# Two fused layers on one core: retention in plain fp32, a later start of layer 2's attention, and differential attention's TensorE work regrouped

## The reference, cut to what matters

```python
# retention, 8 heads, dk 64, dv 128, 4 chunks of 128 positions
def step(state, inp):
    qi, ki, vi = inp
    scores = einsum('bhnd,bhmd->bhnm', qi, ki) * inner_decay
    out = einsum('bhnm,bhme->bhne', scores, vi) + einsum('bhnd,bhde->bhne', qi, state) * q_decay
    state = state * chunk_decay + einsum('bhmd,bhme->bhde', ki * k_decay, vi)
# differential attention, 8 heads, two maps of dk 64, causal, 128 queries a block
s = einsum('bqhjd,bkhjd->bhjqk', qb, kb) - slopes * dist
p = softmax(s); a = p[:, :, 0] - lam * p[:, :, 1]
out = einsum('bhqk,bkhe->bqhe', a, vb)
# layer 2: 8 dilated heads (dk 64) and 8 latent heads (64 + 32), causal, then
mixed = concatenate([o_a * silu(z_a), o_b * silu(z_b)]); out = x + mixed @ w_out
```

## Time and profile before

| | |
|---|---|
| median of 3 runs | 1011.0 us (1006.83 to 1011.19) |
| profiled execution | 1010.72 us, its span 1008.9 us |
| TensorE busy | 966.0 us (96%) |
| VectorE, ScalarE, GpSimd busy | 439.3, 417.3, 479.1 us |
| mean granted TensorE clock | 0.988 |

### The profile page before, as it was taken

How to read it: one execution, slowest core, us unless ns; L and a number is a source line. 1 busy time by engine, 2 the same in 40 slices (tenths; PEclk the granted TensorE clock), 3 DMA queues, 4 the chain that set the end, 5 groups by cost and what they waited for, 6 DMA issues and landing times.

```text
span 1008.9 us, 13340 instructions
## 1 busy us (share of the span) xinstructions
PE 966.0 (96%) x4876; PEld 780.9 (77%) x4876; DVE 439.3 (44%) x1030; ACT 417.3 (41%) x912; POOL 479.1 (47%) x452
## 2 busy tenths in 40 slices
PE   6999998999999999999999999999899979999998
PEld 5777788876888877777767887789788857777777
DVE  3300367323211534567465523325656574456431
ACT  5333453323223344454455332226535354455431
POOL 3543542543446644654434433443457827634342
PEclk9999997999999999999999999999999989999999
DMA  6332210332333322222221241222224311100013
GB/s 212 105 87 82 84 43 1 85 97 70 102 91 101 104 84 67 63 81 64 64 59 47 84 167 63 97 91 80 85 66 132 106 54 50 44 21 22 21 30 117
DMA packets 41168, 78.71 MB, mean 78 GB/s; under 512 B 3296, under 2 KB 5088, under 8 KB 41104
## 3 DMA queue, kind: packets, MB, share of 16 engines
q1 hardware_dynamic: 40240, 76.30, 25.1%
q10 hardware_dynamic: 864, 1.57, 0.6%
HBM read 75.74 MB, written 2.12 MB: 77 GB/s over the span
## 4 chain that ended last, share of the span: by engine, by line
PE 80%; DVE 8%; ACT 4%; issue 3%; POOL 3%; DMA 1%; SPq 1%; ACTq 0%; DVEq 0%; POOLq 0%
PE Z L1671 22%; PE Z L1673 21%; PE Z L1672 20%; PE A L1901 4%; POOL w_lo L858 2%; PE A L1909 2%; PE A L1803 2%; PE A L1816 2%; PE A L1671 1%; DMA raw<-in_w_in 1%; PE A L1681 1%; PE A L1673 1%; PE A L1672 1%; PE A L1869 1%; ACT w_hi L529 1%
## 5 line engine op out<-in xcount | busy, mean ns | idle before, releaser
L858 POOL TENSOR_TENSOR w_lo<-raw,w_hi 128x512 fp32r<-128x512 f32 (+1 forms) x262 | 342.2, 1312 | 422.8 <-ACT w_hi L529 422.5
L1671 PE MATMUL Z<-w_hi,hT_hi 128*128 128x512 f32 (+1 forms) x832 | 339.2, 408 | 10.5 <-POOL w_lo L858 3.9
L1673 PE MATMUL Z<-w_hi,hT_lo 128*128 128x512 f32 (+1 forms) x832 | 324.7, 390 | 0.0
L1672 PE MATMUL Z<-w_lo,hT_hi 128*128 128x512 f32 (+1 forms) x832 | 324.5, 390 | 0.0
L529 ACT CAST w_hi<-raw 128x512 fp32r<-128x512 f32 (+1 forms) x262 | 158.3, 614 | 280.9 <-PE Z L1673 263.9
L1671 PEld LDWEIGHTS Z<-w_hi,hT_hi 128*128 128x128 f32 x832 | 157.0, 189 | 54.8 <-issue 8.8
L1673 PEld LDWEIGHTS Z<-w_hi,hT_lo 128*128 128x128 f32 x832 | 156.8, 188 | 33.0
L1672 PEld LDWEIGHTS Z<-w_lo,hT_hi 128*128 128x128 f32 x832 | 157.4, 189 | 26.7
L1671 PE MATMUL Z<-w_hi,oT_hi 128*128 128x512 f32 x128 | 51.6, 403 | 3.3 <-DVE tmp L1164 2.2
L684 ACT ACTIVATE x_sb<-x_sb,nmax 128x128 f32<-128x128 f32 (+3 forms) x64 | 35.5, 557 | 38.3 <-DVE nmax L1356 38.3
L1673 PE MATMUL Z<-w_hi,oT_lo 128*128 128x512 f32 x128 | 50.1, 391 | 0.0
(11 more groups left out here) (277 smaller groups left out, 1507.5 us busy)
## 6 DMA issues: line engine op xcount, KB each, us to landing
raw<-in_w_in SPq DMA_DIRECT2D x92, 512.0 KB, 3.8
raw<-in_w_out SPq DMA_DIRECT2D x16, 512.0 KB, 3.6
raw<-in_ret_w_o SPq DMA_DIRECT2D x8, 512.0 KB, 3.3
raw<-in_diff_w_o SPq DMA_DIRECT2D x8, 512.0 KB, 3.4
x_sb<-in_x SPq DMA_DIRECT2D x8, 256.0 KB, 5.3
x_sb<-in_x SPq DMA_DIRECT2D x4, 512.0 KB, 6.5
out<-x_sb SPq DMA_DIRECT2D x8, 256.0 KB, 3.3
raw<-in_w_in SPq DMA_DIRECT2D x4, 416.0 KB, 3.2
```

Of the source, the lines that this page charges most:

```text
L858: pool.tensor_tensor(w_lo[:, s % SPLIT_SLOTS, 0:width], raw[:, c % RAW_SLOTS, s - CHUNK_START[c], 0:width], w_hi[:, s % SPLIT_SLOTS, 0:wid ...
L1671: pe.matmul(out, l_hi, r_hi, start=first, stop=False)
L1672: pe.matmul(out, l_hi, r_lo, start=False, stop=False)
L1673: return pe.matmul(out, l_lo, r_hi, start=False, stop=last)
```

## The change

Retention: every split goes away. Turned queries and keys, decayed keys, masked scores, states and values are used as plain fp32, each product is one fp32 `pe.matmul`, `ret_f`, `st_f` and `kd_f` get two buffers, and ACT alone takes the turned queries and keys out of PSUM. Zeros for the query halves are written to two tiles, not four. Layer 2's attention begins after six slots (`ATT_WAIT`), its 71 steps are spread over 52 slots up to slot 57 instead of 57 slots up to slot 56; the six norm pieces move into DVE's steps 3 to 8, and DVE's part of a turned query or key moves to the head of its step. Differential attention: TensorE's step begins with `scores(n+1)`, followed by turn and outputs; the extra yield around `diff_turn` is dropped on all engines, and `diff_due` goes to 72 instead of 86.

```diff
-        return 36 * (v - DIFF_FIRST + 1) // (DIFF_SECOND - DIFF_FIRST)
+        return 29 * (v - DIFF_FIRST + 1) // (DIFF_SECOND - DIFF_FIRST)
     if v < DIFF_THIRD:
-        return 36 + 22 * (v - DIFF_SECOND + 1) // (DIFF_THIRD - DIFF_SECOND)
-    return min(86, 58 + 28 * (v - DIFF_THIRD + 1) // (DIFF_LAST - DIFF_THIRD))
-ATT_STEPS, ATT_SLOTS = 71, 57
+        return 29 + 17 * (v - DIFF_SECOND + 1) // (DIFF_THIRD - DIFF_SECOND)
+    return min(72, 46 + 26 * (v - DIFF_THIRD + 1) // (DIFF_LAST - DIFF_THIRD))
+ATT_STEPS, ATT_WAIT, ATT_SLOTS = 71, 6, 58
 def att_due(v):
-    if v < 0:
+    if v < ATT_WAIT:
         return 0
-    return min(ATT_STEPS, -(-ATT_STEPS * (v + 1) // ATT_SLOTS))
+    return min(ATT_STEPS, -(-ATT_STEPS * (v + 1 - ATT_WAIT) // (ATT_SLOTS - ATT_WAIT)))
...
 # ACT, retention: values, decayed_keys, masked_scores and states are removed
                 def turned_q(p):
                     act.wait_ge(r_t, turn_job("q", p) + 1)
                     for hh in range(2):
                         rows = slice(RDK * hh, RDK * (hh + 1))
-                        act.copy(ret_queries(p)[0][rows, hh, :], A[2][rows, :]).then_inc(r_hi, 1)
+                        last = act.copy(ret_queries(p)[rows, hh, :], A[2][rows, :])
+                    last.then_inc(r_turned, 1)
...
 # DVE, retention: turned_q, turned_k, values and the low parts are removed
-                            if p:
-                                dve.wait_ge(r_plo, 2 * p - 1 + i)
+                            if p > 1:
+                                dve.wait_ge(r_i, 2 * p - 3 + i)
                             dve.wait_ge(r_s, 2 * p + i + 1)
-                            dve.tensor_tensor(ret_f[:, i, :, :, :],
+                            dve.tensor_tensor(ret_f[:, p % 2, i, :, :, :],
...
 # PE, retention (scores; updates, inner and cross products alike)
-                            last = mm3(A[i][:, 256 * (c % 2):256 * (c % 2 + 1)], kT_hi[:, sl, cc], kT_lo[:, sl, cc],
-                                       q_hi[:, :, cc], q_lo[:, :, cc], True, True)
+                            last = pe.matmul(A[i][:, 256 * (c % 2):256 * (c % 2 + 1)], rk[:, p % 2, cc], q[:, :, cc],
+                                             start=True, stop=True)
...
-                    pe.wait_ge(r_slo, po + 1)
+                    pe.wait_ge(r_sf, po + 1)
...
 # DVE, layer 2's attention
                 for n in range(ATT_STEPS):
+                    if n >= 2 and turned_at(n - 2):
+                        att_qk(*turned_at(n - 2))
                     if n < N:
                         scores(n)
...
-                    if n >= 2 and turned_at(n - 2):
-                        att_qk(*turned_at(n - 2))
+                    if 3 <= n < 9:
+                        next(late)
...
 # PE, differential attention
                 for n in range(N + 4):
                     h, i = divmod(n, 4)
+                    if n + 1 < N:
+                        scores(n + 1)
                     if 0 <= n - LAG < N:
                         turn_probs(n - LAG)
                     if 0 <= n - 3 < N and i != 3:
                         outputs(n - 3)
                     yield
                     if i in (1, 2) and h + 1 < H:
                         diff_turn(h + 1, i - 1)
-                        yield
-                    if n + 1 < N:
-                        scores(n + 1)
                     if 0 <= n - 3 < N and i == 3:
                         outputs(n - 3)
                     yield
```

More of the change, by code:

```diff
@@ L596, in turned_q @@
                         rows = slice(RDK * hh, RDK * (hh + 1))
-                        act.copy(ret_queries(p)[0][rows, hh, :], A[2][rows, :]).then_inc(r_hi, 1)
+                        last = act.copy(ret_queries(p)[rows, hh, :], A[2][rows, :])
+                    last.then_inc(r_turned, 1)
                 def turned_k(p):
                     act.wait_ge(r_t, turn_job("k", p) + 1)
[L601 to L609, removed]
-                    if p:
[L611 to L626, removed]
+                    act.activation(rk[:, p % 2, :], A[2][:, :], ACT.Copy, scale=RDK ** -0.5).then_inc(r_turned, 1)
                 pairs = RH // 2
                 if stage == 1:
+                    act.wait_ge(q_zeros, 2)
                     turned_q(0)
@@ L1232, in scale_heads, with retention @@
                     dve.tensor_tensor(o, o, r, ALU.mult).then_inc(o_normed, 1)
[L1234 to L1241, removed]
-                def turned_k(p):
-                    dve.wait_ge(r_khalf, p + 1)
-                    dve.scalar_tensor_tensor(kT_lo[:, p % 2, :], A[2][:, :], RDK ** -0.5, kT_hi[:, p % 2, :],
-                                             ALU.mult, ALU.subtract).then_inc(r_lo, 1)
-                def values(p):
-                    vh, vl = ret_values(p)
-                    dve.wait_ge(r_vhi, p + 1)
-                    dve.tensor_tensor(vl, z_ret[:, :, 1024 + 256 * p:1280 + 256 * p], vh, ALU.subtract).then_inc(r_v, 1)
+            def retention():
                 def states(p):
                     dve.wait_ge(r_u, p + 1)
-                    if p:
-                        dve.wait_ge(r_slo, p)
+                    if p > 1:
+                        dve.wait_ge(r_x, 2 * (p - 1))
+                    st = st_f[:, p % 2, :, :]
                     for c in range(3):
@@ L1280, in retention @@
                 pairs = RH // 2
-                if start:
-                    turned_q(0)
-                    turned_k(0)
-                    values(0)
-                    return
                 for p in range(pairs + 1):
@@ L1297, in retention @@
                                               ALU.mult).then_inc(r_pf, 1)
[L1298 to L1307 removed]
                     if p == 0:
[L1309 to L1311 removed]
+                        states(p)
                     if p:
@@ L1433, in query_zeros, with attention @@
                     last.then_inc(q_zeros, 1)
-            def attention():
+            def attention(late):
                 ph, N = ATT2, 8 * H
@@ L1477, in attention, with att_slot @@
                     yield
-            def att_slot(g, k, steps, gates, late):
+            def att_slot(g, k, steps, gates):
                 v = TT * (KD * (g - G_ATT2) + k)
                 for t in range(TT):
-                    if v + t < 6:
-                        next(late)
                     if 30 <= v + t < 36:
@@ L1591, in _ @@
             dve.engine_nop().then_inc(cols_ready, 1)
-            steps, steps2, gates, late = diff(), attention(), take_gates(G_ATT2, 2), late_norms()
+            steps, steps2, gates = diff(), attention(late_norms()), take_gates(G_ATT2, 2)
             norms = {G_DIFF0 + 2: head_scale(HEAD_NORM[G_DIFF0 + 1]), G_DIFF0 + 3: head_scale(HEAD_NORM[G_DIFF0 + 2]),
@@ L1628, in _ @@
                     dve.engine_nop().then_inc(lam_dots, 1)
-                    for part in (*ret_queries(0), *ret_queries(1)):
+                    for part in (ret_queries(0), ret_queries(1)):
                         for hh in range(2):
@@ L1640, in _ @@
                                       ALU.add).then_inc(row_ready, 1)
-                if g == G_RET0:
-                    retention(start=True)
                 if g == G_RET:
@@ L1648, in _ @@
                     dve.wait_ge(row_out, 16)
-                    retention(start=False)
+                    retention()
                 if g == G_LAT:
@@ L1770, in retention @@
                             cc = slice(P * c, P * (c + 1))
-                            last = mm3(Z[2 + hh][:, cc], q_hi[:, hh, cc], q_lo[:, hh, cc],
-                                       st_hi[:, c - 1, :], st_lo[:, c - 1, :], True, True)
+                            last = pe.matmul(Z[2 + hh][:, cc], q[:, hh, cc], st_f[:, po % 2, c - 1, :], start=True, stop=True)
                         last.then_inc(r_x, 1)
```

124 lines of the change are left out of this document (34 added, 90 removed).

## The result

Before 1008.9 us (median of 4), after 1028.6 us (median of 4, 1027.9 to 1033.4): ratio 1.021, 95% interval 1.016 to 1.025. The forecast was 991 (984 to 1001). The profiled execution took 1028.5 us (span 1026.7). Parts A and B together take off 19.4 us against 17.7 forecast; part C, forecast at -2.7, costs 37.9.

What follows compares the result with a forecast made beforehand. The prediction took one nearly always full in-order TensorE queue as the bound, except at retention's end and layer 2's attention start. Its sum was 1010.7 - 14.7 - 3.0 - 2.7 = 990.3, said as 991, range 984 to 1001.

Steps and rivals of the forecast that it cites:

- Part A: Retention unsplit into single fp32 matmuls: -12.3 us at its end and -2.4 of clock behind it, -14.7; bounds -7 and -17.
- rival 3: Retention: fp32 matmuls of 256 columns cost like 512, +14 us, giving 1004; chance 0.03.
- rival 1: Retention's end: clock falls again or the tail stays on turns and copies, saving only 7 to 8 us, 998; chance 0.19.
- Part B: Layer 2's attention six slots later, with its VectorE and GpSimd reordering: -3 us; bounds +2 and -7.
- the slots that I priced at -3.6: Layer 2's attention start: idle 8.1 us against 7.4, but 12 slots done instead of 6, worth 4.5; net -3.6.
- the order of VectorE's query parts, priced at -0.5: Layer 2's attention: VectorE's query parts ahead of the scores help some key turns, -0.5 us.
- The 3.1 us in the turn of set 4: Layer 2's attention: TensorE waits up to 3.1 us there because GpSimd's first latent piece stands before set 4's scaling.
- Part C: Differential steps in one go, scores first on TensorE: -2.7 us; bounds +1 and -5.
- The +0.5 for the turn behind the low part: Differential stage: a query or key turn has one gap, not two, to the next turn of probabilities; +0.5 us.
- The term of -2.2: Differential stage: in 22 steps scores and turns share one excursion from the projection, saving 0.10 us each, -2.2.
- The -1.0: Differential stage: the second half's first key turn, waiting 1.5 us for z_sb, comes a slot or two later; -1.0 us.
- Rival 4: Differential stage: after 14 query and key turns the turn of probabilities waits for VectorE's low part, +32 us, 1022; chance 0.04.

Runs made afterwards that it cites:

- e10: e6 with layer 2's attention starting at slot 0 again over 57 slots, other edits of that attention kept: 990.8 us.
- e11: e6 with VectorE's low parts of layer 2's turned queries and keys back behind the row maximum and copy of the step: 995.2 us.
- e1: The changed kernel with the old differential step put back on every engine, the retention and layer 2 edits kept: 990.7 us.
- e6: The changed kernel with its pace of 72 half steps, but the scores back in the second half step, behind the query or key turn: 989.6 us.
- e7: The changed kernel with only VectorE's order changed: row maximum of set n+1 at the end of its first half step n, ahead of the low part: 996.4 us.
- e8: e7 with TensorE's first half step ordered turn, outputs, then scores of set n+1: 1001.7 us.
- e12: e6 with GpSimd's last six latent pieces one in a step from step 16 on, instead of two in each of steps 16 to 18: 988.3 us.

## Why the prediction was wrong, by its own steps

**Part A, -14.7 forecast, -14.5 measured.** The timeline of TensorE in retention's end after, for the earlier trace rows:

```profile
134.04 1.89 PE L1612 MATMUL A<-rq,rk 128*128 128x256 f32 x8
135.76 1.95 PE L1657 MATMUL Z<-z_ret,ret_f 128*128 128x128 f32 x16
137.55 0.60 PE L1599 MATMUL A<-ident,z_ret 128*128 128x128 f32 x4
...
141.19 0.70 PE L1626 MATMUL A<-z_ret,kd_f 128*128 128x256 f32 x2 [0.40 <-ACT rq L589]
...
148.87 0.70 PE L1626 MATMUL A<-z_ret,kd_f 128*128 128x256 f32 x2 [0.40 <-ACT rq L589]
...
158.43 0.50 PE L1573 MATMUL Z<-w_hi,hT_hi 128*128 128x512 f32 x1 [0.78 <-DVE o_sb L1228]
```

Four fp32 matmuls of 256 columns take 135.76 - 134.04 = 1.72, so 0.43 each (I took 0.45: rival 3 is out); eight of 128 columns take 1.79, 0.22 each. The hand-made schedule forecast waits of 0.4, 0.4 and 1.1; they are 0.40, 0.40 and 0.78. The end takes 24.4 (forecast 25.2), and the clock held: rival 1 is out. That the medians agree to 0.2 is partly luck: the windows give 37.5 - 24.4 = 13.1 at the end and 2.4 behind it, 15.5 in all. And the prediction's "agrees" for 0.223 rests on no row at 128 columns, where the fp32 matmul takes only twice the 0.11 of an fp32r one; at 512 columns it does take four times as long, 0.95 against 0.23.

**Part B, -3 forecast, -4.9 measured, for the wrong reason.** The waits at its start were right: 1.36 and 0.23 for Z2 and Z3, 3.00 for q_lo. But the slots that I priced at -3.6 are worth about 1, within the spread (e10), and the order of VectorE's query parts, priced at -0.5, is worth 5.5, as much as the whole of B (e11). (By its own terms, 8.1 - 7.4 - 4.5, the -3.6 should read -3.8. Part A's bound with the clock falling as before is -6.3 by its terms, not -7.) The 3.1 us in the turn of set 4 was a misreading of the diff: GpSimd's latent pieces begin in its step 10, not ahead of the scaling of set 4. They cost 2.3 + 0.8 = 3.1 later, where two pieces stand ahead of one scaling. GpSimd's timeline, then TensorE's:

```profile
875.62 2.66 POOL L890 TENSOR_TENSOR m_sb<-z_sb,lam_v 128x512 f32<-128x512 f32 x2
878.38 0.58 POOL L936 TENSOR_SCALAR sgd_sb<-sgd_sb,rinv 128x384 f32<-128x384 f32 x1
```

```profile
879.02 0.55 PE L1805 MATMUL A<-ident,sgd_sb 128*128 128x128 f32 x3 [1.36 <-POOL sgd_sb L936]
```

That the sign agreed, and the size roughly, is chance.

**Part C, -2.7 forecast, +37.9 measured: the step that failed.** It was "Scores leave half a step earlier, so exp, the weight copies queued behind it on ACT, and w_lo behind those wait less". I followed who is served earlier and not what the scores themselves wait for, so their wait for the row maximum stood in the sum at nothing. The runs showed 29.0 us of it, 27.7 more idle time over the same work, and 11.2 of busy time at a lower clock on top. The one wait for a row maximum in the stage before, 0.4 us, showed only that the old place was late enough; how late it had to be was in the same trace, in the time at which each row maximum ends. The +0.5 for the turn behind the low part looked at the right chain (1.8 us of turn, copy, low part), but the scores meet it first, with a row maximum of 0.7 to 1.3 added and norms between. In the 12 waits behind a low part at most four instructions stand between it and the row maximum that ends them.

The term of -2.2 had its count right and its price wrong. From the first scores to the last outputs TensorE returns to the projection 80 times in e1, 66 in e6 and 57 in the changed kernel and in e7, each return with 0.32 instead of 0.23 to the next matmul: 23 returns for the 22 forecast, which would be 2.1 us. But TensorE's busy time for that work is 193.0 in e1, with one slot of 0.7 more in it, 192.4 in e6 and 191.6 in e7, so 0.7 us is all that shows. The -1.0 held: the wait of 1.5 for z_sb is 0.3 in e6 and gone in the changed kernel.

**The rivals.** Rival 4 had the right sign and stage and a size of the right order (+32), and it named VectorE behind with other work; it named the wrong waiting instruction (e8 shows that one, 5.6 us). It got 0.04 because the stage before was idle for only 3.5 us and VectorE busy for half of it. Both rows were true and no evidence: e7 has the same VectorE work as the changed kernel and 26.4 us less of waits at the scores. No other rival had part C costing time.

**The version that beats both.** e6 (989.6), or e12 (988.3): parts A and B with TensorE's old order, 1.8% under the kernel before and 3.8% under the changed one.

## What to carry to other kernels

When an instruction is moved earlier in a full in-order queue, write down each thing that it waits for and walk the producer's queue up to it: everything that stands there between the old and the new place, with its own waits, becomes idle time of the full engine and of all that is queued behind. A stage with almost no idle time says that the present order has enough slack, not how much; the old trace says how much, in the time between the end of what an instruction waits for and the place to which it moves (511.55 against 508.90 above). Move the work that frees the bank first (here VectorE's row maximum), and only then the producer's.

## What was not expected of the hardware

The waits cost clock as well. After the wait of 3.34 us at 412.49 the projection's matmuls start 0.43 apart, and 0.23 apart again from 417.2 on; the chain of work that ended last and the window:

```profile
412.49 0.62 PE A L1700 x6
...
414.31 0.43 PE Z L1573
414.74 0.43 PE Z L1574
...
417.23 0.24 PE Z L1574
```

```profile
414.00:417.00 3.00, 3.00 (x9) 2.42 (x9) 2.69 (x13) 0.00 (x0) 0.00 (x0) 0.50 0.45 163
```

The granted clock there is 0.50, the lower level, 1.2 GHz. There are eight such falls in the stage, each of some 3 us and each behind a wait at the scores: 3.34 at 412.49, 2.20 at 429.91, 2.31 at 448.00, 1.54 at 497.36, 2.48 at 511.64, 3.44 at 522.66, 3.09 at 532.63 and 1.96 at 548.81. The wait of 2.49 at 465.46 was followed by none (1.00 in 460 to 480), nor was one of 1.54 at 557.28, so the length of the wait alone doesn't decide. Behind the two waits of 1.54:

```profile
499.00:502.00 3.00, 3.00 (x9) 2.41 (x9) 1.34 (x7) 1.40 (x5) 1.04 (x1) 0.50 0.01 3
557.20:561.00 3.80, 3.72 (x22) 2.93 (x22) 2.03 (x8) 1.22 (x5) 1.42 (x2) 1.00 0.48 133
```

The falls make the 11 us of busy time, so each microsecond of wait cost 1.4 in the end. Fp32 matmuls of 128 and 256 columns with gaps of 0.4 kept the full clock through all of retention's end, where three times as many fp32r ones had lost it.
